# Spreading the front of a merged attention and expert kernel by TensorE time, and moving expert sums to VectorE beside it

## What is computed

```
h = rmsnorm(x); z = h @ w_in
x = x + concat[GLA(z_gla), FoX(z_fox)] @ w_out     # linear attention, 8 heads of forgetting attention
x = x + PEER(rmsnorm(x))

PEER, per frame and each of 8 heads: top 16 of 128 x 128 product keys -> expert numbers idx, weights g
  u = u_tab[idx]; a = gelu(u . h)                  # 128 gathered rows of 1024 for one frame
  y = sum over the 128 of (g * a) * v_tab[idx]
```

## Time and profile before

| | |
|---|---|
| median of 3 runs | 3928.57 us (3922.43 to 3935.04) |
| the profiled execution | 3929.12 us, its span 3927.5 us |
| from the first dot to the end | 902.2 to 3927.5 us |
| busy: PE, DVE, ACT, POOL | 79%, 66%, 30%, 33% of the span |
| gathers | 1056, of 1131.10 MB in all, a median of 11.8 us from issue to landing |
| rows added by TensorE and by VectorE | 800 and 256 |
| mean granted TensorE clock | 0.88 of full speed |

### The profile page before, as it was taken

The page is one execution under the profiler, slowest core; times in us unless marked ns, Lnnn a source line. Parts: engine busy times, 40 slices in busy tenths (PEclk is TensorE's granted clock), DMA queues, the critical chain, the costliest instruction groups (busy, mean ns, idle before and its releaser), DMA issues.

```text
span 3927.5 us, 33430 instructions
## 1 busy us (share of the span) xinstructions
PE 3116.0 (79%) x9089; PEld 1656.2 (42%) x9089; DVE 2581.0 (66%) x6288; ACT 1163.9 (30%) x2530; POOL 1308.2 (33%) x1145
## 2 busy tenths in 40 slices
PE   5999999776786788777789777798877778866767
PEld 3665556463343335333345333344533333532322
DVE  2432334228768766898765898865698776577874
ACT  1222232212432343222353322344222223322211
POOL 0000000003444433444443444433344443344443
PEclk9778877778898899988899988899998889988889
DMA  3010000089999999999999999998999998899998
GB/s 160 25 41 22 22 24 26 17 309 377 412 420 415 404 403 376 420 413 406 401 397 362 400 418 401 396 379 317 401 418 414 399 415 348 349 420 416 410 417 347
DMA packets 187364, 1267.87 MB, mean 323 GB/s; under 512 B 23381, under 2 KB 24238, under 8 KB 39606
## 3 DMA queue, kind: packets, MB, share of 16 engines
q0 software_dynamic: 159488, 1131.10, 71.1%
q1 hardware_dynamic: 25350, 122.09, 7.9%
q10 hardware_dynamic: 2352, 12.72, 0.8%
HBM read 1238.95 MB, written 26.88 MB: 322 GB/s over the span
## 4 chain that ended last, share of the span: by engine, by line
PE 33%; DMA 21%; DVE 13%; issue 7%; ACT 5%; POOL 1%; DVEq 0%; SPq 0%; ACTq 0%; POOLq 0%
PE ps_acc L1295 21%; DMA uv_ring<-in_peer_uv,expert_index 20%; DVE uv_ring L1493 5%; PE ps_scores L1270 4%; PE ps_scores L1238 3%; DVE v_sums L1501 2%; PE ps_scores L1151 2%; ACT coef_diag L1110 2%; PE ps_fox_o L1169 1%; DVE key_top_index L1383 1%; PE ps_turn L1162 1%; DVE key_scores_rest L1384 1%; ACT L1019 1%; PE ps_acc L1139 1%; PE ps_scores L1152 1%
## 5 line engine op out<-in xcount | busy, mean ns | idle before, releaser
L1295 PE MATMUL ps_acc<-uv_ring,coef_diag 128*128 128x512 f32 x3200 | 1736.0, 690 | 680.1 <-ACT coef_diag L1110 679.7
L983 POOL DMA_INDIRECT uv_ring<-in_peer_uv,expert_index x1056 | 1260.5, 1194 | 1756.9 <-PE ps_acc L1295 1623.1
L1493 DVE CUSTOM_DVE_ANT_0 uv_ring<-uv_ring,h_rows 128x1024 f32<-128x1024 f32 x1056 | 1286.9, 1221 | 309.5 <-DMA uv_ring<-in_peer_uv,expert_index 306.0
L1295 PEld LDWEIGHTS ps_acc<-uv_ring,coef_diag 128*128 128x128 f32 x3200 | 663.6, 219 | 1618.6 <-ACT coef_diag L1110 924.8
L1102 ACT ACTIVATE gelu_u_dot_h<-u_dot_h 128x2 f32<-128x2 f32 x528 | 107.3, 203 | 1370.2 <-DVE u_dot_h L1493 1368.7
L389 PE MATMUL ps_z<-w_in,x_T 128*128 128x512 f32 x864 | 397.6, 619 | 0.0
L1110 ACT ACTIVATE coef_diag<-ident_f,coefficients 128x128 f32<-128x128 f32 x768 | 279.1, 395 | 332.0 <-DVE coefficients L1485 331.6
L1501 DVE SCALAR_TENSOR_TENSOR v_sums<-uv_ring,coefficients,v_sums 128x1024 f32<-128x1024 f32 x256 | 327.6, 1280 | 0.0
L1270 PE MATMUL ps_scores<-weight_chunk,rows_T 128*128 128x256 f32 x1152 | 261.9, 381 | 0.7 <-issue 0.7
L389 PEld LDWEIGHTS ps_z<-w_in,x_T 128*128 128x128 f32 x864 | 169.2, 200 | 206.6 <-issue 206.6
L1270 PEld LDWEIGHTS ps_scores<-weight_chunk,rows_T 128*128 128x128 f32 x1152 | 220.1, 191 | 61.0 <-issue 34.3
(11 more groups left out here) (206 smaller groups left out, 2648.0 us busy)
## 6 DMA issues: line engine op xcount, KB each, us to landing
weight_chunk<-scratch_keys_w SPq DMA_DIRECT2D x48, 1024.0 KB, 9.1
weight_chunk<-in_w_out_chunks SPq DMA_DIRECT2D x24, 1024.0 KB, 13.3
uv_ring<-in_peer_uv,expert_index POOLq DMA_INDIRECT x1056, 11.8
w_in<-in_w_in SPq DMA_DIRECT2D x8, 1548.0 KB, 24.6
uv_ring<-in_w_peer_q_T SPq DMA_DIRECT2D x8, 1024.0 KB, 22.7
x_T<-in_x_T POOLq DMA_DIRECT2D x9, 512.0 KB, 3.8
x_rows<-in_x_rows POOLq DMA_DIRECT2D x9, 512.0 KB, 4.6
x_mid<-in_x_rows SPq DMA_DIRECT2D x9, 512.0 KB, 16.3
```

Source lines behind the costliest of these rows:

```text
L983: pool.indirect_dma_start(out=ring[:, s % RING, :], out_offset=None, in_=dram["uv"], in_offset=bass.IndirectOffsetOnAxis(ap=idx[:, t % IDX ...
L1295: mm = pe.matmul(acc[:, c, :], diag[:, r, :], ring[:, r, D + c * 512:D + (c + 1) * 512], start=first, stop=False, skip_group_check=True)
L1493: dve.tensor_tensor_reduce(out=ring[:, s % RING, 0:D], in0=ring[:, s % RING, 0:D], in1=h2[:, t % 2, :], scale=1.0, scalar=0.0, op0=ALU.mul ...
```

## The change

The steps get other weights, meant as TensorE time in us: attention of tile t weighs 13 + 7.5 t (t at most 7.5) over its 33 steps, a projection column 3.5, other projection steps 1.5, a routing step 0.45. Before, attention and projection steps weighed 2 and routing steps 1. Weight not used up by whole steps is now carried from slot to slot, so that a slot may issue no step. `BESIDE[s]` tells whether the front stands in attention or projection after slot s. Where it does, VectorE takes one row of every group, else one of every second group as before; tile 8's groups stay with none.

```diff
-    weight, due = [], []
+    weight, due, on_pe = [], [], []
     for ts in BATCHES:
-        weight += [2] * (ATT_STEPS * len(ts) + out_steps(ts))
+        for t in ts:
+            weight += [(13.0 + 7.5 * min(t, TILES - 0.5)) / ATT_STEPS] * ATT_STEPS
+        weight += [3.5] * (OUT_CH * len(ts)) + [1.5] * (out_steps(ts) - OUT_CH * len(ts))
         base = len(weight)
+        on_pe += [True] * (base - len(on_pe))
         due += [(base, SLOTS * t - 12) for t in ts if t]
-        weight += [1] * route_steps(ts)
+        weight += [0.45] * route_steps(ts)
+        on_pe += [False] * route_steps(ts)
...
-    upto, f = [], first
+    upto, at_work = [], total[first]
     for s in range(NS):
-        ahead = [(total[g] - total[f]) / (at - margin - s) for g, at in due if at - margin > s and g > f]
-        goal = total[f] + (max(ahead) if ahead else len(weight))
-        g = f
-        while g < len(weight) and total[g] < goal:
-            g += 1
-        f = g
-        upto.append(f)
-    return first, upto, len(weight)
+        ahead = [(total[g] - at_work) / (at - margin - s) for g, at in due if at - margin > s and total[g] > at_work]
+        at_work += max(ahead) if ahead else total[-1]
+        upto.append(max(f for f in range(len(total)) if total[f] <= at_work + 1e-6))
+    beside = [f < len(on_pe) and on_pe[f] for f in upto]
+    return first, upto, len(weight), beside
...
 def on_vector(g):
 
     if GRP * g >= SLOTS * TILES:
         return 0
-    return g % 2
+    return 1 if BESIDE[GRP * g + GRP] else g % 2
```

More of the change, by code:

```diff
@@ L712, in front_plan @@
     first = max(f for f, s in due if s <= margin + 4)
-    upto, f = [], first
+    upto, at_work = [], total[first]
     for s in range(NS):
-        ahead = [(total[g] - total[f]) / (at - margin - s) for g, at in due if at - margin > s and g > f]
-        goal = total[f] + (max(ahead) if ahead else len(weight))
-        g = f
-        while g < len(weight) and total[g] < goal:
-            g += 1
-        f = g
-        upto.append(f)
-    return first, upto, len(weight)
-PROLOGUE, UPTO, FRONT = front_plan()
+        ahead = [(total[g] - at_work) / (at - margin - s) for g, at in due if at - margin > s and total[g] > at_work]
[3 more added lines that the diff above has]
+    return first, upto, len(weight), beside
+PROLOGUE, UPTO, FRONT, BESIDE = front_plan()
 def on_vector(g):
```

## The result

The changed kernel takes 3906.39 us (median of six runs, 3901.64 to 3915.1), the kernel before 3927.86 us beside it: a ratio of 0.9944 (0.9927 to 0.9961). It is faster by 0.4 to 0.7%, where 1.7% was forecast, and it lies 1.4 us outside the stated range. The profiled execution took 3905.69 us, its span is 3904.1 us.

The account below looks back on a forecast made before the run. Transfers at 418 GB/s were taken to set the pace, stopping beside attention. From 3927.5 us, minus 79 for attention, plus 10 for denser routing, gave 3858.5 us of span, 3860 us executed; range 3826 to 3905 us.

Parts of the forecast that it names:

- the bound: Whole kernel: transfers set the pace at 418 GB/s; 157 us lost in all, 103 us in the attention stretches.
- spreading: Attention and projection get 519 slots in place of 332; loss there falls from 103 to 24 us, gain 79 us.
- Deadlines: Stored x of tiles 6, 7 and routed heads: room of 15 and 13 slots suffices, costing nothing.
- The drain: Last 48.5 us, when no gathers are left: its loss stays 17 us.
- denser routing: Tiles 2 to 5, 37 steps in 16 slots: 2.80 us a slot on VectorE; 10 us charged, 30 us more at 2.90.
- the prediction's own sign of being wrong: Dense routing: rates under 395 GB/s there would show the prediction wrong.
- The third rival: VectorE paces denser routing and tiles 2, 3: 2.90 us a slot, +30 us, 45 us left in attention; 3901 us, chance 0.13.
- The attention's residue: 519 attention and projection slots: 24 us still lost, from tile 1's 0.04 us a slot at one step a slot.
- The moved rows: 132 rows to VectorE beside attention: 169 us more work there, covered by transfers with 0.4 us a slot to spare.
- The held issue: Gather issues held by VectorE's added row sums: up to 169 us more, 4029 us; chance 0.03, nothing charged.

Follow-up runs that it names:

- early scores: Changed kernel with TensorE's key scores of each head but a batch's first issued 6 front steps earlier: 3863.2 us; same edit in the kernel before: 3911.84 us.
- weight 0.6: Changed kernel with a routing step weighed 0.6 in place of 0.45: 3886.93 us, 0.9901 to the kernel before.
- The floor: Changed kernel plus key scores 6 steps ahead, no VectorE rows in routing, attention steps weighing at least 1.1: 3845.07 us; also with 132 rows back on TensorE: 3831.34 us.
- the plan alone: Changed kernel's new weights with the old rows, VectorE keeping one row of every second group: 3912.5 us, 0.9958 to the kernel before.
- the rows alone: Kernel before, old plan, with one row of every group on VectorE in attention and projection: 3914.18 us, 0.9962 to the kernel before.
- no sums in routing: Changed kernel with VectorE adding no rows where the front routes, TensorE taking them: 3864.39 us, 0.9833 to the kernel before.

## Why the prediction was wrong

The direction and the bound were right. Transfers at 418 GB/s set the pace, the attention stretches were where they stopped, and spreading brought most of it back: 69 us against 79 forecast. VectorE's busy time beside 6 and 7 came out as worked out (2.06 us a slot, 2.05 forecast); TensorE had 1.99 us a slot and not 1.76, which cost nothing. Deadlines cost nothing: POOL again waited for a stored x only once, at the start (103.0 us). The drain was 5 us cheaper than taken.

**The step that failed** is the one on denser routing. It took VectorE's slot as busy time plus 0.18 us, 2.80 in all, with 2.90 as the upper end, and charged 10 us. The busy time was right (2.62 forecast, 2.60 and 2.61 measured). The 0.18 came from a stretch of 61 steps in 32 slots, where late scores cost 3.6 us, and I carried it over to 74 steps unchanged. But the wait depends on density: TensorE issues a head's scores 4 front steps ahead of VectorE's use, which is 2 slots at 2 steps a slot and 1.7 at 2.3. By the plan all 32 heads of the two stretches had two slots before, and eight of them have one now. The wait went from 0.11 to 0.29 us a slot (0.25 in the routing of 2, 3), and a slot to 2.93 and 2.97 us. The two stretches lost 59 us in place of the 26.5 of the sum: 32 of the 45.6 us by which the forecast span was too short (3858.5 against 3904.1). The rates there, 383 and 380 GB/s, were the prediction's own sign of being wrong (under 395). The early scores, which give 46 us back by the ratios with VectorE's work unchanged, show it, and so does weight 0.6, which takes the wait away by density alone. The distance is not all of it: worked out head by head from the timeline, the eight heads with one slot wait 3.2 us each, but the 24 with two wait 1.5, where they waited 1.0 before. What adds to those was not traced.

The third rival had the place right and set VectorE at 2.90 us a slot, near the 2.93 and 2.97 measured; its price, 30 us, is 27 by its own terms (0.19 x 229 - 16.5), and some 42 were measured. It had 45 us left in attention, where 34 were. The two errors cancel, so that its 3901 us lies 5 us from the median by luck.

I had the same mechanism in hand on the other side. For the attention I argued by the distance from scores to maximum in slots, and took the gain from making it longer; for the routing I did not ask what making it shorter does. The row that would have told was the start of the kernel before, some 80 steps in the first 32 slots, 6.9 us lost. I set it aside as a matter of chunk loads. VectorE's waits for key scores in its first 41 slots (902 to 1027 us, 394 GB/s) are 14.6 us, 0.36 a slot. With early scores the same slots run at 420 GB/s under either plan (902 to 1019 us of the old plan, 901 to 1019 us of the new one): it was the scores, not the chunks.

**The attention's residue** was 34 us, not 24. The nearest row that I took, tile 1's attention at one step a slot, does not stand for tile 1 after the change, which runs at 1.5: in the kernel before these slots (1027 to 1145 us) moved 417 GB/s and lost 0.3 us, after it 9.4. TensorE had less to do there after the change (84 of 119 us busy, 97 of 118 before), so its load is not what costs here. The plan weighs work and not latency, so it made the light tile's attention denser. The floor, which spaces the same steps out again, removes the loss (1.3 us).

**The moved rows** I kept at no cost with thin cover; in the changed kernel that held. But I also gave them a share in the gain, and on top of the spread they have none that can be told: the plan alone gives 0.9958 and the rows alone 0.9962, together 0.9944. With attention at about half a step a slot TensorE has room for three rows of four.

**The held issue** (rival) did not grow. The mean issue of a gather is 1194 ns before and after, with 132 more row sums on VectorE:

```profile
L985 POOL DMA_INDIRECT uv_ring<-in_peer_uv,expert_index x1056 | 1260.8, 1194 | 1736.5 <-PE ps_acc L1297 1552.6
```

The rule of the Trainium skill, SBUF — State Buffer, the two separate sides, may well be what stretches single issues; no run here tests it. In this kernel it is not worse for the change, and all of POOL's work is 2% of the chain that ended last (1% before). The Trainium skill, DMA: Bandwidth & Descriptors, where 436 GB/s comes from, has about 358 GB/s as binding between HBM and SBUF; the same page, section Measured, gives that as the share of a core whose neighbour streams too, and 425 GB/s for one core alone. This kernel runs on one core, and attention of 6 and 7 went from 357 to 411 GB/s, so 358 was no limit here.

**Left open.** Why the moved rows cost 14 us with the floor (0.9792 to 0.9756, intervals apart) and nothing without it (0.9799 and 0.9798) is settled only as to place. The profiled executions with the floor are 11 us apart. 6 us of it are beside tiles 6 and 7 and 4 beside 2 and 3; with the rows, then without them:

```profile
1299.00:1570.00 271.00, 195.05 (x598) 101.08 (x596) 192.27 (x315) 100.89 (x196) 111.89 (x96) 0.84 0.99 402
2543.00:2971.00 428.00, 319.65 (x961) 159.73 (x962) 321.70 (x503) 135.03 (x275) 186.57 (x158) 0.84 0.99 407
...
1298.00:1565.00 267.00, 220.74 (x692) 113.42 (x691) 164.06 (x291) 107.10 (x218) 115.38 (x97) 0.92 0.99 409
```

Without the floor the rows cost 2 us beside 6 and 7 (425 and 423 us), and pay for it beside tile 1 (10 us lost with them, 14 without) and tile 8 (268 us with them, 275 without). The plan is the same beside 6 and 7 with and without the floor, so some of this is the scatter of single executions; the rest was not traced to a wait.

## What to carry to other kernels

When engines run one interleaved order, a spread has two prices at each stretch: the busy time per slot, and the distance in slots between a producer's step and its consumer's. Changing density changes both, so give a producer its lead in slots (or time) and not in steps before making a stretch denser, and don't let a plan by work run light steps closer together than their latency. Slots taken from one stretch make another denser; look there for the loss.

An in-order engine's work and waits add up; compare their sum with the pace of the transfers. Here taking away either one was enough to bring most of the loss back.

Price a change as a ledger of lost transfer time, stretch by stretch, and fill in the stretches that pay for it with the same care as those that gain.

## What the runs showed of the hardware

TensorE's granted clock fell where it was given less to do: beside attention of 6 and 7 it is 0.86 with 311 us busy in 421, and 0.93 with 356 busy in the same 421 us when the rows are its own. Part of the relief is so given back as slower matmuls (one matmul of a row's sum takes 720 ns in the mean of the whole run, and 684 when the rows are its own), since the clock is at one of two levels (1.2 and 2.4 GHz) and spends more of the time at the lower. In 1039 to 1156 us of the kernel with weight 0.6 it was 0.75, with 85 of 117 us busy.

One core alone moved 416 GB/s over 470 us of 8 KB gathers, and 420 over 118 us, at a DMA share of 1.01.

A stretch whose work and producer waits stay below the transfers' time in the mean can still lose: with no sums in routing VectorE's busy time and key-score waits make 2.32 + 0.32 = 2.64 us a slot in 2237 to 2563 us (115 slots), under 2.7, and the slot took 2.83. The waits come in lumps of up to 5.2 us, behind which 14.3 us of waits for gathers follow. That the ring of eight slots is too short to hide such a lump fits this, but no run changed the ring.
